# Normalization in setup, seeded expert sums and gate tiles inside the recurrence, in a two-block transformer kernel

## The reference, cut to what matters

```python
def first_block(x, ...):
    h = layer_norm(x, ln_in_g, ln_in_b)
    m = gated_mixer(h, ...)                       # ... @ w_out
    h = layer_norm(ALPHA * h + m, ln1_g, ln1_b)   # ALPHA = 2 ** 0.25
    f = moe_ffn(h, ...)                           # sum over 4 experts of gate_w * (a @ w_exp_out[e] + b_exp_out[e])
    return layer_norm(ALPHA * h + f, ln2_g, ln2_b)

def second_block(x, ...):
    h = x @ w_in                                  # q, k, v ... and the gates nsa_z, sb_z, hg_z
    o_hg = hgrn2_mixer(hg_q, hg_f, hg_i, lb)
    o_hg = o_hg * rsqrt(mean(o_hg ** 2) + eps) * hg_norm_w
    mixed = concat([o_nsa * silu(nsa_z), o_sb * silu(sb_z), o_hg * silu(hg_z)])
    return layer_norm(ALPHA * x + mixed @ w_out, ln_g, ln_b)
```

## Time and profile before

| | us |
|---|---|
| three runs | 2269.96, 2270.13, 2276.75 |
| median | 2270.13 |
| the profiled execution | 2272.07 |
| its span in the trace | 2270.3 |
| TensorE busy | 2041.3 (90%) |
| VectorE busy | 1691.3 (74%) |
| ScalarE busy | 1249.8 (55%) |
| GpSimd busy | 298.7 (13%) |

### The profile page before, as it was taken

The page is one execution under the profiler, slowest core; times in us unless marked ns, Lnnn a source line. Parts: engine busy times, 40 slices in busy tenths (PEclk is TensorE's granted clock), DMA queues, the critical chain, the costliest instruction groups (busy, mean ns, idle before and its releaser), DMA issues. The chain is left out here.

```text
span 2270.3 us, 29884 instructions
## 1 busy us (share of the span) xinstructions
PE 2041.3 (90%) x10236; PEld 1644.9 (72%) x10236; DVE 1691.3 (74%) x1990; ACT 1249.8 (55%) x1397; POOL 298.7 (13%) x172
## 2 busy tenths in 40 slices
PE   3988989974999999999999999999983879889878
PEld 2767768763788888888888888888872757676766
DVE  5463671266899999999999999999995366535775
ACT  3342432322677777777777777777770344343541
POOL 0202114201021211112111121111210000000000
PEclk9998999996999999999999999999996988699999
DMA  5212133525899999999999999999983611011211
GB/s 195 56 51 80 45 73 89 182 104 196 316 370 394 376 384 384 377 393 372 388 381 374 395 372 389 381 372 398 370 305 89 144 19 38 12 35 56 57 57 75
DMA packets 201620, 519.03 MB, mean 229 GB/s; under 512 B 21974, under 2 KB 81502, under 8 KB 201196
## 3 DMA queue, kind: packets, MB, share of 16 engines
q1 hardware_dynamic: 191212, 482.68, 57.4%
q0 software_dynamic: 9504, 34.61, 5.9%
q10 hardware_dynamic: 832, 0.80, 0.1%
HBM read 494.41 MB, written 29.41 MB: 231 GB/s over the span
## 5 line engine op out<-in xcount | busy, mean ns | idle before, releaser
L1721 DVE TENSOR_TENSOR piece_lower<-piece,moe_upper 128x2048 fp32r<-128x2048 f32 x384 | 870.2, 2286 | 30.1 <-ACT moe_upper L1641 30.1
L1641 ACT CAST moe_upper<-piece 128x2048 fp32r<-128x2048 f32 x384 | 734.1, 1914 | 282.1 <-PE bank L1573 270.3
L1571 PE MATMUL bank<-moe_upper,x_hi 128*128 128x512 f32 x1536 | 620.9, 404 | 2.5 <-DVE x_hi L1715 2.5
L1573 PE MATMUL bank<-moe_upper,x_hi 128*128 128x512 f32 x1536 | 606.8, 395 | 0.0
L1572 PE MATMUL bank<-piece_lower,x_hi 128*128 128x512 f32 x1536 | 602.3, 392 | 0.0
L1571 PEld LDWEIGHTS bank<-moe_upper,x_hi 128*128 128x128 f32 x1536 | 290.5, 189 | 68.3 <-DVE piece_lower L1721 2.9
L1572 PEld LDWEIGHTS bank<-piece_lower,x_hi 128*128 128x128 f32 x1536 | 290.4, 189 | 63.3
L1573 PEld LDWEIGHTS bank<-moe_upper,x_hi 128*128 128x128 f32 x1536 | 290.0, 189 | 62.9
L1526 POOL DMA_INDIRECT mixed<-moe_y,moe_dst x32 | 104.7, 3273 | 27.5 <-issue 27.5
L135 PE MATMUL bank<-x_hi,ahead_lower 128*128 128x512 f32 x256 | 103.5, 404 | 0.0
L1524 POOL COPY moe_dst<-row 128x1 uint32 (+1 forms) x32 | 6.7, 209 | 618.7 <-ACT moe_y L1630 618.7
(11 more groups left out here) (557 smaller groups left out, 3430.8 us busy)
## 6 DMA issues: line engine op xcount, KB each, us to landing
piece<-in_w_exp_in_dram SPq DMA_DIRECT2D x256, 1024.0 KB, 7.4
piece<-in_w_exp_out_dram SPq DMA_DIRECT2D x128, 1024.0 KB, 9.4
ahead<-in_w_in_dram SPq DMA_DIRECT2D x19, 512.0 KB, 4.2
ahead<-in_w_in_dram SPq DMA_DIRECT2D x3, 2048.0 KB, 8.0
ahead<-in_w_in_dram SPq DMA_DIRECT2D x4, 1536.0 KB, 6.8
merge_raw<-in_w_in_dram SPq DMA_DIRECT2D x8, 512.0 KB, 5.8
ahead<-in_w_out_dram SPq DMA_DIRECT2D x2, 2048.0 KB, 8.0
out_w<-in_w_out_dram SPq DMA_DIRECT2D x2, 2048.0 KB, 8.3
```

Of the source, the lines that this page charges most:

```text
L1571: nc.tensor.matmul(to, hi[:, f, :], upper[u][:, t, cols], start=f == 0 and not biased, stop=False)
L1573: done = nc.tensor.matmul(to, lo[:, f, :], upper[u][:, t, cols], start=False, stop=f == NK - 1)
L1641: nc.scalar.copy(upper[h % SPLIT][:, :, :], ring[s][:, :, :]).then_inc(hi_ready, 1)
L1721: nc.vector.tensor_tensor(lower[s][:, :, :], ring[s][:, :, :], upper[h % SPLIT][:, :, :].bitcast(F32), ALU.subtract).then_inc(lo_ready, 1)
```

## The change

In plain words, in the order of the program:

- The statistics' variance, the deviation, the inverse and the four normalized tiles move from "ln0" into the setup stage; `layer_norm_stage` gets `done=NT` and skips them.
- The merge stage zeroes one tile of `mixed` (the spare rows) in place of five.
- The route stage loads the output biases, ScalarE copies them and scales the four tiles of `x` by `ALPHA` in place, SyncE stores these to `mixed`, and VectorE computes the biases' remainder and the shares. GpSimd waits for the stores after its first two gathers. The experts' scatters then add onto `ALPHA * x`.
- The combine stage has no biases to load, no shares to compute and no `ALPHA * x + mixed`; it adds `mixed` and the bias product at once.
- In the recurrence's stage TensorE projects the rest of gate tile 4 and tile 5 after the last products, SyncE loads the weights of tiles 6 and 7, and tile 6's weights are split at the end.
- "hgt" projects only tiles 6 and 7, gates only tile 4, loads `w_out` without a wait, and splits four of the eight tiles of `w_out`'s lower part.
- "out2" splits the other four, gates tile 5 besides 6 and 7, and multiplies five tiles first (60 matmuls), then three (36).

The diff, cut to its core:

```diff
 layer_norm_stage:
+            if done < NT:
                 rows.variance(dve, done, NT).then_inc(var_ready, 1)
                 dve.wait_ge(std_ready, stds + 1)
                 rows.inverse(dve, done, NT)
 setup_stage, scalar:
             act.drain().then_inc(t5_ready, 1)
+            act.wait_ge(var_ready, 1)
+            rows.deviation(0, NT).then_inc(std_ready, 1)
 setup_stage, vector:
                 statistics(nc, k, i)
+            dve.drain()
+            rows.variance(dve, 0, NT).then_inc(var_ready, 1)
+            dve.wait_ge(std_ready, 1)
+            rows.inverse(dve, 0, NT)
+            dve.wait_ge(gain_in, 16)
+            dve.wait_ge(shift_in, 16)
+            for i in range(NT):
+                rows.row(dve, i).then_inc(normed, 1)
 merge_stage, sync:
-            for i in range(NT + 1):
-                sp.dma_start(k.mixed[i * P:(i + 1) * P, :], zeros[:, :]).then_inc(mixed_zeroed, 16)
+            sp.dma_start(k.mixed[S:S + P, :], zeros[:, :]).then_inc(mixed_zeroed, 16)
 route_stage, sync (before and behind the loads of the first 8 pieces):
+            for g in range(3):
+                sp.dma_start(full[NE * g:NE * g + NE, :], A["b_exp_out"][0]).then_inc(bias_in, 16)
...
+            for i in range(NT):
+                sp.wait_ge(x_scaled, i + 1)
+                sp.dma_start(k.mixed[i * P:(i + 1) * P, :], k.x[:, i, :]).then_inc(k.row_stored, 16)
 route_stage, scalar:
+            act.wait_ge(bias_in, 48)
+            nc.scalar.copy(r.out_bias[:, :], full[:, :]).then_inc(bias_hi, 1)
+            for i in range(NT):
+                nc.scalar.activation(k.x[:, i, :], k.x[:, i, :], ACT.Copy, scale=ALPHA).then_inc(x_scaled, 1)
             act.wait_ge(top_ready, 1)
 route_stage, vector:
+            dve.wait_ge(bias_hi, h0 + 1)
+            split_lower(nc.vector, full[NE:2 * NE, :], r.out_bias[NE:2 * NE, :], r.out_bias[NE:2 * NE, :])
             dve.wait_ge(br_in, 16)
             dve.wait_ge(logits_ps, 1)
...
             nc.vector.tensor_copy(total[:, 0:1], ends[:, NE - 1:NE])
+            nc.vector.tensor_tensor(pick[:, :, :, :], pick[:, :, :, :],
+                                    r.weight[:, :, :].unsqueeze(3).to_broadcast([P, NT, TOPK, NE]), ALU.mult)
+            dve.drain()
+            nc.vector.tensor_reduce(r.share[:, :, 0, :], pick[:, :, :, :].rearrange("p i c e -> p i e c"), AX.X, ALU.add)
+            dve.drain()
+            nc.vector.tensor_copy(r.share[:, :, 1:3, :], r.share[:, :, 0:1, :].to_broadcast([P, NT, 2, NE]))
             dve.wait_ge(listed, 1)
 experts_stage, gpsimd:
                 gather(1, 1)
+                pool.wait_ge(k.row_stored, 32 + 16 * NT)
 combine_stage, vector (bias loads, bias copy, shares, bias remainder and residual removed):
+            for i in range(NT):
                 dve.wait_ge(mixed_in[i], 16)
                 for c in range(2):
                     dve.wait_ge(biased, 2 * i + c + 1)
-                    nc.vector.tensor_tensor(x[:, i, cols], x[:, i, cols], k.bank[7 - 2 * i - c][:, :], ALU.add)
+                    nc.vector.tensor_tensor(x[:, i, cols], mixed[:, i, cols], k.bank[7 - 2 * i - c][:, :], ALU.add)
 hgrn_stage, sync:
+            sp.wait_ge(arg_ready, N)
+            for f in range(Z_EARLY, NK):
+                sp.dma_start(rest_tile(z.raw_rest, f), column_tiles(A["w_in_2"][0], Z_FIRST[f])).then_inc(z.loaded[4], 16)
 hgrn_stage, tensor (behind the output products):
+            project(Z_BETWEEN, 1)
+            project(Z_EARLY - 1, 0)
+            project(Z_EARLY - 1, 1)
 hgrn_norm_stage, sync:
-            sp.wait_ge(z.ps, Z_EARLY)
             load_ahead(sp, k, column_tiles(A["w_out_2"][0], 0, 512))
 hgrn_norm_stage, tensor:
-            project(Z_BETWEEN, z.w[Z_BETWEEN], range(4, NK))
-            project(Z_EARLY - 1, z.w[Z_EARLY - 1], range(NK))
+            project(Z_EARLY)
             pe.wait_ge(ready, n + 1)
...
-            for f in range(Z_EARLY, NK):
-                pe.wait_ge(z.lo, f + 1)
-                project(f, Split(z.upper[f % 2][:, :, :], lowers[f - Z_EARLY]), range(NK))
+            project(Z_EARLY + 1)
 output_stage:
-        split = 0 if z is None else Z_EARLY
+        split = 0 if z is None else M_SPLIT          # 5
+            if z is not None:
+                output_lower(nc, dve, k, range(W_LOWER, NK), z.lo)      # W_LOWER = 4
```

156 lines of the change are left out of this document (67 added, 89 removed).

## The result

The changed kernel takes 2241.10 us (median of 4 runs, 2239.36 to 2245.08), the kernel before, in runs on the same chip, 2270.05 us (median of 4, 2265.12 to 2276.75). The ratio is 0.9879, with a 95% interval of 0.9866 to 0.9893. The profiled execution took 2245.08 us with a span of 2243.3; that of before took 2272.07 with 2270.3.

A forecast was written before the change was run, and what follows sets the result against it. TensorE, VectorE and DMA fill the experts; elsewhere dependency chains and stage seams bind. Terms -5.6 + 2.1 - 6.7 - 13.0 = -23.2 took the profiled 2272.07 to 2248.9 us, median forecast 2247, range 2243 to 2256.

The forecast's parts named there:

- Start: Setup and first normalization: the first x_hi copy comes at 28.4 in place of 34.02, 5.6 us less.
- Merge: Merge stage: four of five zero stores go, nobody on the chain waits for them, so no time changes.
- Route: Route stage: the shares join VectorE's chain ahead of the experts, 2.1 us more; other added work is hidden.
- so all of it counts: Route stage: the three share operations, 2.15 us, lie in the chain that starts the experts and add their full time.
- Combine: Combine stage: shares, bias work and the ALPHA * x addition leave; first row load or bias product late next; 6.7 us less.
- Recurrence and tail: Recurrence stage, "hgt" and "out2": earlier w_out load and moved matmuls, "out2" at full clock; 13.0 us less.
- the other branch: Start of "out2": the clock falls as before, so the tail gains 11.2 us; as a rival 2249 us, chance 0.14.
- the slower rival: Experts' loop: lengthens through scatters onto ALPHA * x rows and other buffer addresses; 2293 us at 4%, chance 0.03.
- the table load's: Start: ScalarE is held behind each table load as long again, 1.3 us more, 2248 us; chance 0.08.
- the recurrence's: Recurrence stage: ScalarE's chain, waiting for VectorE, ends 3 us behind TensorE, 2250 us; chance 0.11.
- Everything behind shifts: After the start: all later work moves earlier by the full 5.6 us, bounds 4.6 and 6.0.
- It lies 1.9 above the median of the runs: Sum: the profiled run before, 2272.07 us, exceeds the median 2270.13, so 2248.9 becomes 2246.9 for the median.

The follow-up runs named there:

- the 24 products: 24 products with unused results added in the last unit of the second block's attention, in four kernels: kernel before 2256.55 us, changed kernel 2232.78 us.
- the one with the shares twice: Changed kernel with the shares computed twice in the route stage and one more VectorE drain per combine tile: 2252.54 us in its one run.
- The late load: Changed kernel with the load of the first half of w_out_2 put behind gate tile 6 of the last stage but one: 2250.77 us, ratio 0.9912.
- shares moved, twelve products: Changed kernel with shares at VectorE's experts end, twelve unused products before the experts' transposes, lam sums and exponentials in setup: 2241.73 us, ratio 0.9868.

## Why the prediction was right and where it was wrong

- **Start:** right, 5.35 us for 5.6. With the 24 products the part measures 6.1.
- **Merge:** nothing, as predicted. The 1.15 us ahead of the route stage are spread over five stages, 0.3 to 0.5 in each; the kernels that left these stages alone differ from each other by as much.
- **Route:** the shares' 2.13 us were right, the step "so all of it counts" was wrong. 1.4 to 1.7 us come back at the start of the loop, since the clock's rise did not move with the work. Both kinds of kernel show it, eight traces with the shares in the route stage (79.3 to 79.8 us from gather to first output) against nine without (80.6 to 81.3); the one with the shares twice, 80.4, does not fit a rise that stands still. What fits all eighteen is the number of products started at half clock in both stretches: 11 to 14 in the eight, in which the second stretch is 3.4 us long, 20 to 23 in the nine and 18 in the one, in which it is 6.8. Why the second stretch is long or short is not shown.
- **Combine:** right in what is late next, the first row load; the term of 6.7 was 7.8. The rest is in about equal parts the first load's landing, 3.68 us after the stage's start where I took 4.4 although the shortest of the earlier trace rows is 3.6, and the drain that each of four tiles loses, 0.15 us.
- **Recurrence and tail:** right in mechanism and nearly in size (13.8 for 13.0), the clock of the output stage with it. The late load shows what the other branch would have cost. That the fall of before came from its gap of 2.46 us is only half right: behind 2.44 us it did not come, but behind the 0.56 to 0.59 us of the ten traces with the tail part and an early load it never did.
- **The loop:** unchanged, 1092.67 and 1092.46 us from the first scaled output to the last scatter; the slower rival did not come. Nor did the table load's, nor the recurrence's.
- **What failed is the step under all of them: "Everything behind shifts".** In its terms these are the route's "so all of it counts" and the combine stage's first load and drains; apart from the terms it is the step from the profiled run to the median, "It lies 1.9 above the median of the runs". In the two traces the forecast's 2248.9 was 3.8 us too high: 1.9 in the experts, 1.15 ahead of the route, 1.1 in the combine stage and 0.8 in the tail, less 0.7 lost in the second block and 0.4 at the start and in the route. The 0.7 lie ahead of the attention, 81.87 us at a mean clock of 0.81 in place of 81.07 at 0.84. The other 2.1 us lie between the profiled runs and the medians: I subtracted the 1.9 by which the run of before stood above its median, and that of after stood 4.0 above its own. Where a median leaves out what its trace shows, the trace can't say why; the attention stage of the second block, 142.6, 146 or 152 us in untouched code, is a likely place. Of the unprofiled runs only the mean granted clock was measured, 0.950 to 0.951 in those of after against 0.948 in the profiled one, and it does not say in which stage, so the cause of these 2.1 us stays open. With the attention's clock held up by the 24 products the change is worth 23.8 us by the medians and 29.5 by the traces, against a sum of 23.2. That the sum is so near the first is in part luck, since the terms were off in both directions.

## What to carry to other kernels

Sum the terms of a change, but ask of every wait behind it whether the clock in the next stage is set by your work or by something that does not move with it: here 1.4 of 2.1 us came back, and 6 us went in a stage nobody had touched. When parts measured alone don't add up to the whole, compare stage lengths between traces before you believe in an interaction, and look whether the trace is of a usual run: the times here differ by several us between runs of one kernel. And look for stretches where TensorE is the bound at half clock once it has less work there: some products nobody reads made the stage 10 us shorter.

## What was not expected of the hardware

- The attention stage with 24 products more (24 times 0.23, 5.5 us of TensorE at full clock) is shorter, 135.7 us for 146.0. In its last unit TensorE was busy 42.29 of 44.00 us at half clock without them and 37.97 of 43.00 at full clock with them.
- In seventeen of the eighteen traces the clock rose in the experts 37.5 us after it had fallen in the route stage, with the first gather 2.2 us earlier or later; with the shares twice it was 41.0. In one of the seventeen (shares moved, twelve products) it also came up for 3.4 us before that, in the added products.
- Behind idle gaps of TensorE of 2.1 to 2.5 us the clock fell in four traces and stayed up in three, the longest of these with a gap of 2.44 us.
- A table load of 1.28 us was followed by its activation after 0.02 us.
